# A relative-position bias table in SBUF: loaded at another place in GpSimd's queue, straight into its own buffer

## The chip, the core and the metric

The kernel runs on one core of one Trainium2 chip. The time is device microseconds (us) of one execution of the whole program; a measurement gives the median of several runs. The engines are TensorE (PE; its weight loads are PEld), VectorE (DVE), ScalarE (ACT), GpSimd (POOL) and SyncE (SP), each with its own instruction stream, tied together by semaphores. DMAs are issued by SP (queue q1 in the profile) and by GpSimd (queue q0), and both are carried by the same 16 DMA engines of the core.

## What is computed

One decoder block on x of 256 tokens x 1024: a normalised input is projected by `w_in`, two token mixers run in parallel on the projections, and their outputs are gated, merged and projected again. The change touches the bias of the second mixer:

```
dist_own = qpos[:, None] - (own_start + offs)[None, :]
s_own = einsum('bhcd,bhkd->bhck', qc, k_own) + bias_hb[:, t5_bucket(dist_own)][None]
s_own = where(dist_own >= 0, s_own, NEG_INF)
```

The bias of head h for query i and key j depends on i - j alone. So a row of 384 values for each head (`bias_rows` in DRAM, with -1e30 where i < j) holds all of it, and partition p of the table is that row from element p on: 256 ascending values, which have to be read from the last to the first to be in the order of the keys.

The first mixer (gated DeltaNet, 8 heads) needs, for every head and each of two chunks of 128 tokens, the inverse of a unit lower-triangular matrix; its blocks of 32 x 32 are solved by a substitution on DVE, over all heads at once.

## The kernel before

**Tiles.** All weights go through four slots (`raw`, `w_hi`, `w_lo`, each 128 x 1024). A tile is 512 KB. SP loads it into `raw` (L387), ACT rounds it to `w_hi` (L636), DVE makes the remainder `w_lo` (L865), and PE multiplies in three thirds: high by high, high weight by low input, low weight by high input (L1274 for most tiles, L1292 for the value tiles), some 0.96 us a third. One counter S numbers the thirds of the whole program, tile n having S = 3n, 3n+1, 3n+2; every engine's program is unrolled along S by hand, so each engine works strictly in the order that its own code has.

**Loads.** Tiles are loaded in pairs: SP waits for `s_lo` before an even tile n, that is until `w_lo` of tile n-3 is made, and then issues n and n+1. ACT casts tile n+2 during part 1 of tile n (`split_hi`), DVE makes its `w_lo` in part 2 (`split_lo`). Tiles 0 to 15 are key (K) and value (V) tiles; a K tile is fetched in rows of 512 B.

**Around the change.** For each key tile, ACT copies the product (L687), DVE adds three taps (L938), ACT takes the tanh (L690), DVE finishes `kT_all` (L951); then `key_tokens(j)` lets PE transpose it (L1340) and ACT square and copy it (L699, L701). `key_tokens(j)` on PE waits until ACT has copied that of j-1 (`s_k0`). At S = 26 to 33 ACT runs `decay`, 16 exponentials over `th_E` (L678); at S = 28 to 39 `similarity` on PE (L1351) and DVE (L964) writes `la_all`, which is the memory of `xin`.

**GpSimd.** It stores the bias rows (L539) and the decay rows (L541) to DRAM, loads the bias table into `xin` under the name `climbing` (L544, 1 MB), loads the decay rows broadcast to all partitions into `th_E` in two halves (L548, 512 KB each), computes the norms of the first keys, masks the first half of `th_E` (L495), copies `climbing` with reversed columns into `bias` (L555), and masks the second half. DVE waits for that copy (`s_bias`) before its first write of `la_all`. Later GpSimd stores and loads the blocks of the substitution (L504, L513), computes the value norms (L488), and waits for the substitution's end (L569). The table is first read by DVE at L1043 and L1045 in `stage_a` of head 0, at S = 99.

Of the kernel before, what the change touches and what calls it, by code (L numbers as in the profile page):

```python
# [31 lines left out]
P = 128  # L32
HALF = P // 2
D = 1024
SEQ = 256
NC = SEQ // P
KT = D // P
HEADS = 8
# [3 lines left out]
SCALE = float(P) ** -0.5  # L42
# [45 lines left out]
BIAS_W = 384  # L88
# [20 lines left out]
def build(nc, x, norm_pre_w, w_in, b_gate, conv_w, dn_a_log, dn_dt_bias, dn_onorm_w, rel_bias, w_branch, w_out,  # L109
          norm_post_w, consts, onehot, out):  # L110
    with ExitStack() as ctx:
        def sb(name, shape, dt=F32):
            return ctx.enter_context(nc.sbuf_tensor(name, shape, dt))

        def sem(name):
            return ctx.enter_context(nc.semaphore(name))
# [3 lines left out]
        bA, bB, bC, bD, bE, bF = bank[2:]  # L120
# [4 lines left out]
        xin = sb("xin", [P, NC, D])  # L125
# [13 lines left out]
        bias = sb("bias", [P, HEADS, SEQ])  # L139
# [33 lines left out]
        sc = sb("sc", [P, BIAS_W])  # L173
# [19 lines left out]
        E_all = th_E[:, late:late + HEADS, :].rearrange("p h (c n) -> p h c n", c=NC)  # L193
        E_flat = th_E[:, late:late + HEADS, :].rearrange("p h n -> p (h n)")
        la_all = xin[:].rearrange("p c n -> p (c n)").rearrange("p (h c n) -> p h c n", h=HEADS, c=NC)
        climbing = xin[:].rearrange("p c n -> p (c n)").rearrange("p (h n) -> p h n", h=HEADS)
        m2, m32 = acc, tacc[:, 0, :]
        squares = T_all[:].rearrange("p h c n -> p (h c n)")[:, 0:512]
        post = vtok_all[:, 0, :]
# [5 lines left out]
        bias_rows = nc.dram_tensor("bias_rows", [HEADS, BIAS_W], F32, kind="Internal").ap()  # L205
# [31 lines left out]
        s_M_in2 = sem("s_M_in2")  # L237
        s_M_out2 = sem("s_M_out2")
        s_G_p = sem("s_G_p")
        s_M_in = sem("s_M_in")  # L240
# [15 lines left out]
        s_bias = sem("s_bias")  # L256
        s_bias_p = sem("s_bias_p")
        s_brow = sem("s_brow")
        s_climb = sem("s_climb")
        s_cst = sem("s_cst")  # L260
        s_d_p = sem("s_d_p")
        s_f = sem("s_f")
# [10 lines left out]
        s_hT = sem("s_hT")  # L273
# [63 lines left out]
        s_stored = sem("s_stored")  # L337
# [99 lines left out]
        def _(pool):  # L437
# [47 lines left out]
            def value_norms(q):  # L485

                heads = slice(2 * q, 2 * q + 2)
                pool.tensor_tensor(tab[:, 2:4, heads], tk[:, 0, :, heads], power[:, 0], ALU.pow).then_inc(s_vn, 1)  # L488
                pool.wait_ge(s_vn, q + 1)

            def mask_decay(half):

                pool.wait_ge((s_E_in, s_E_in2)[half], 16)
                part = E_all[:, 4 * half:4 * half + 4].rearrange("p h c n -> p (h c) n")
                pool.affine_select(part, part, [[0, 4 * NC], [1, P]], ALU.is_ge, NEG_INF, base=0,  # L495
                                   channel_multiplier=-1).then_inc(s_Em, 1)
                pool.wait_ge(s_Em, half + 1)
# [41 lines left out]
            pool.dma_start(bias_rows, brow).then_inc(s_stored, 16)  # L539
            pool.wait_ge(s_grow, 1)  # L540
            pool.dma_start(g_rows, grow[:]).then_inc(s_g_out, 16)  # L541
            pool.wait_ge(s_stored, 16)
            pool.wait_ge(s_hT, KT)
            pool.dma_start(climbing, bass.AP(bias_rows.tensor, 0, [[1, P], [BIAS_W, HEADS], [1, SEQ]])).then_inc(s_climb, 16)  # L544
            pool.wait_ge(s_g_out, 16)
            for half in range(2):
                size = HEADS * SEQ // 2
# [3 lines left out]
            pool.wait_ge(s_tab, 2)  # L551
            norms(0)
            mask_decay(0)
            pool.wait_ge(s_climb, 16)
            pool.tensor_copy(bias[:], climbing[:, :, SEQ - 1::-1]).then_inc(s_bias, 1)  # L555
            pool.wait_ge(s_bias, 1)
            mask_decay(1)
            norms(1)
            norms(2)
# [4 lines left out]
            load_blocks(1)  # L564
            for q in range(HEADS // 2):
                value_norms(q)
            pool.wait_ge(s_sub, 2 * STEPS)
            for a in range(2):
                pool.dma_start(bass.AP(t_blocks.tensor, BLK * a, [[BLK * BLK, HALF], [2 * BLK, BLK // 2], [1, BLK]]),  # L569
# [286 lines left out]
        def _(ve):  # L856
            v = nc.vector
# [30 lines left out]
            for k in range(KT):  # L888
                ve.wait_ge(s_h_hi, k + 1)
                v.scalar_tensor_tensor(out=h_lo[:, k, :], in0=bank[k][:, 0:SEQ], scalar=vec[:, R_PRE + k:R_PRE + k + 1],  # L890
                                       in1=h_hi[:, k, :].bitcast(F32), op0=ALU.mult, op1=ALU.subtract).then_inc(s_h_lo, 1)
# [61 lines left out]

            def similarity(j):

                if j == 0:
                    ve.wait_ge(s_bias, 1)
                if j % 2 == 0:
                    ve.wait_ge(s_sig, j + 1)
                ve.wait_ge(s_E, 2 * j + 2)  # L960
                ve.wait_ge(s_G_p, j + 1)
                for c in range(NC):
                    ps = (bA, bC)[j % 2][:, P * c:P * c + P]
                    v.scalar_tensor_tensor(out=la_all[:, j, c, :], in0=ps, scalar=tab[:, c, j:j + 1],  # L964
                                           in1=E_all[:, j, c, :], op0=ALU.mult, op1=ALU.mult).then_inc(s_la, 1)
# [64 lines left out]
            def stage_a(g, s):  # L1030
                at = at2[:, g % 2]
                if s == 14:
                    ve.wait_ge(s_A_p, g + 1)
                    if g >= 2:
                        ve.wait_ge(s_o1_p, g - 1)
                    v.tensor_tensor(at, chunks(bA[:, 0:256]), E_all[:, g], ALU.mult).then_inc(s_A, 1)
                elif s == 15:
                    ve.wait_ge(s_sc_p, g + 1)
                    if g == 0:
                        ve.wait_ge(s_bias, 1)  # L1040
                    if g:
                        ve.wait_ge(s_pt_p, g)
                    v.scalar_tensor_tensor(out=sc[:, 0:256], in0=bC[:, 0:256], scalar=SCALE, in1=bias[:, g, :],  # L1043
                                           op0=ALU.mult, op1=ALU.add).then_inc(s_sc, 1)
                    v.scalar_tensor_tensor(out=sc[:, 256:384], in0=bC[:, 256:384], scalar=SCALE, in1=bias[:, g, P:2 * P],  # L1045
                                           op0=ALU.mult, op1=ALU.add).then_inc(s_sc, 1)
                    ve.wait_ge(s_sc, 2 * g + 1)
                    v.tensor_reduce(mx[:, 0:1], sc[:, 0:256], AX_X, ALU.max).then_inc(s_mx, 1)
                    ve.wait_ge(s_sc, 2 * g + 2)
                    v.tensor_reduce(mx[:, 1:2], sc[:, 256:384], AX_X, ALU.max).then_inc(s_mx, 1)  # L1050
                    ve.wait_ge(s_mx, 2 * g + 2)
                    v.tensor_scalar(mx[:, 2:4], mx[:, 0:2], -1.0, None, ALU.mult).then_inc(s_nmx, 1)
                elif s == 18:
                    ve.wait_ge(s_pexp, 2 * g + 2)
                    v.reciprocal(mx[:, 6:8], mx[:, 4:6]).then_inc(s_rsum, 1)
                elif s == 25:
                    ve.wait_ge(s_pv_p, g + 1)
                    ve.wait_ge(s_gz, 2 * g + 2)
                    if g:
                        ve.wait_ge(s_ylo_b, g)  # L1060
                    v.scalar_tensor_tensor(out=y32[:, 1, :], in0=bA[:, 0:SEQ], scalar=0.5, in1=gzb[:],
                                           op0=ALU.mult, op1=ALU.mult).then_inc(s_yb32, 1)
                elif s == 27:
                    ve.wait_ge(s_yhi_b, g + 1)
                    v.tensor_tensor(y_lo[:, 1, g:g + 1, :], one(y32[:, 1, :]),
                                    y_hi[:, 1, g:g + 1, :].bitcast(F32), ALU.subtract).then_inc(s_ylo_b, 1)
# [66 lines left out]
            for S in range(3 * BRANCH0):  # L1133
                n, part = S // 3, S % 3
# [19 lines left out]
            with ve.Fori(0, KT // 2) as i:  # L1154
                for t in range(4):
# [4 lines left out]
                    if t % 2 == 0:  # L1160
                        ve.wait_ge(s_m_hi, d + 1)
                    v.scalar_tensor_tensor(out=one(m2[:, t % 2, :]), in0=(th_a if t % 2 else th_b)[:, bass.ds(d, 1), :],
                                           scalar=1.0, in1=one(bank[t % 2][:, 0:SEQ]), op0=ALU.add,
# [11 lines left out]
            for c in range(NC):  # L1175
# [7 lines left out]
                for e in range(2):  # L1183
                    cols = slice(512 * e, 512 * e + 512)
                    v.scalar_tensor_tensor(out=res[:, c, cols], in0=res[:, c, cols], scalar=tiny[:, 30 + c:31 + c],
                                           in1=raw[:, c, cols], op0=ALU.mult, op1=ALU.add).then_inc(s_o_f, 1)
# [350 lines left out]
```

## Time and profile before

| | us |
|---|---|
| median of 3 runs (375.31 to 375.71) | 375.61 |
| the profiled execution, its own time | 374.69 |
| its span in the trace | 372.9 |
| busy: PE / PEld | 359.8 / 344.8 |
| busy: DVE / ACT / POOL | 268.9 / 219.2 / 62.4 |
| granted TensorE clock, mean | 0.994 |

The trace counts from its first record; 1.8 us of the execution's own time lie outside the span. A line such as L636 is line 636 of the kernel. Busy time of an engine is that of its instructions, without the issuing of DMAs on SP. The granted clock is given in parts of 2.4 GHz: 1.00 is 2.4 GHz, 0.50 is 1.2 GHz.

### The profile page before, as it was taken

The numbers are of one execution on the slowest core, as the hardware profiler recorded it, in microseconds if no ns is written. First come the engines' busy times: TensorE is split into PE (matmuls) and PEld (weight loads), VectorE is DVE, ScalarE is ACT, GpSimd is POOL, SyncE is SP. The second block draws the span as 40 slices with busy tenths as digits, with TensorE's granted clock in tenths as the row PEclk, the third lists the DMA queues.
The fourth block names the chain that finished last, engine by engine and source line by source line (L and its number), as shares of the span: only waits on it lengthen the run. The fifth ranks groups of instructions, "written<-read, shape, count | busy, mean of one in ns | idle before, by whom it ended". The sixth has DMA issues, their size and how long they took to land.

```text
span 372.9 us, 7655 instructions
## 1 busy us (share of the span) xinstructions
PE 359.8 (96%) x2755; PEld 344.8 (92%) x2755; DVE 268.9 (72%) x558; ACT 219.2 (59%) x500; POOL 62.4 (17%) x121
## 2 busy tenths in 40 slices
PE   8999599999999999999999999999999999999993
PEld 6788597799999999999999999999999999999882
DVE  2966595479966887878878878688786557667644
ACT  5783696444556566767666586666676643534531
POOL 3544415550033000202020201001020100000000
PEclk9999899999999999999999999999999999999999
DMA  8849645976787654484447544466446565765533
GB/s 259 219 129 284 200 146 147 239 199 152 190 228 186 173 150 114 124 212 120 114 119 193 143 112 115 122 179 153 112 117 182 155 183 156 212 208 199 224 116 113
DMA packets 99343, 62.45 MB, mean 167 GB/s; under 512 B 3652, under 2 KB 94190, under 8 KB 99310
## 3 DMA queue, kind: packets, MB, share of 16 engines
q1 hardware_dynamic: 98014, 58.59, 56.9%
q0 software_dynamic: 1296, 3.43, 3.2%
q8 instruction: 20, 0.33, 0.4%
q14 instruction: 13, 0.11, 0.1%
HBM read 60.41 MB, written 1.59 MB: 166 GB/s over the span
## 4 chain that ended last, share of the span: by engine, by line
PE 88%; DMA 4%; ACT 4%; DVE 2%; issue 1%; POOL 1%; DVEq 0%; POOLq 0%; ACTq 0%
PE banks L1274 63%; PE banks L1491 6%; PE banks L1292 4%; DMA raw<-in_w_in_dram 3%; ACT th_E L678 1%; PE banks L1374 1%; PE banks L1259 1%; PE banks L1381 1%; PE banks L1392 1%; DMA xin<-in_x_dram 1%; PE banks L1430 1%; PE banks L1219 1%; ACT junk L699 1%; PE banks L1433 1%; PE banks L1437 0%
## 5 line engine op out<-in xcount | busy, mean ns | idle before, releaser
L865 DVE TENSOR_TENSOR w_lo<-raw,w_hi 128x1024 fp32r<-128x1024 f32 x102 | 124.5, 1223 | 37.6 <-ACT w_hi L636 37.4
L636 ACT CAST w_hi<-raw 128x1024 fp32r<-128x1024 f32 x103 | 106.6, 1045 | 13.2 <-DMA raw<-in_w_in_dram 7.8
L1274 PE MATMUL banks<-h_lo,w_hi 128*128 128x256 f32 x568 | 83.1, 289 | 0.0
L1274 PE MATMUL banks<-h_hi,w_lo 128*128 128x256 f32 x568 | 82.8, 289 | 0.0
L1274 PE MATMUL banks<-h_hi,w_hi 128*128 128x256 f32 x568 | 82.1, 287 | 0.3 <-PE banks L1292 0.3
L1274 PEld LDWEIGHTS banks<-h_hi,w_hi 128*128 128x128 f32 x568 | 72.7, 191 | 1.4 <-issue 1.4
L1274 PEld LDWEIGHTS banks<-h_lo,w_hi 128*128 128x128 f32 x568 | 73.5, 193 | 0.0
L1274 PEld LDWEIGHTS banks<-h_hi,w_lo 128*128 128x128 f32 x568 | 73.3, 192 | 0.0
L938 DVE SCALAR_TENSOR_TENSOR acc<-banks,vec,acc 128x255 f32<-128x255 f32 (+2 forms) x72 | 34.5, 479 | 6.0 <-ACT acc L734 3.3
L586 POOL TENSOR_TENSOR so<-so,rnq 128x2 f32<-128x2 f32 x8 | 3.8, 471 | 148.8 <-ACT junk L801 148.8
L845 ACT CAST h_hi<-tacc 128x256 f32 x8 | 3.2, 406 | 28.4 <-DVE tacc L1167 28.4
L742 ACT ACTIVATE tz<-banks 128x256 f32<-128x256 f32 x16 | 6.1, 384 | 22.7 <-PE banks L1274 22.7
L1274 PE MATMUL banks<-y_hi,w_hi 128*128 128x256 f32 x128 | 18.0, 283 | 0.0
L1274 PE MATMUL banks<-y_lo,w_hi 128*128 128x256 f32 x128 | 18.0, 283 | 0.0
L1274 PE MATMUL banks<-y_hi,w_lo 128*128 128x256 f32 x128 | 18.0, 283 | 0.0
L1274 PEld LDWEIGHTS banks<-y_hi,w_hi 128*128 128x128 f32 x128 | 16.5, 192 | 0.0
L1274 PEld LDWEIGHTS banks<-y_hi,w_lo 128*128 128x128 f32 x128 | 16.5, 192 | 0.0
L1274 PEld LDWEIGHTS banks<-y_lo,w_hi 128*128 128x128 f32 x128 | 16.5, 192 | 0.0
L734 ACT ACTIVATE acc<-banks,vec 128x256 f32<-128x256 f32 x16 | 7.6, 473 | 15.0 <-PE banks L1274 14.9
L1491 PE MATMUL banks<-w_hi,h_hi 128*128 128x512 f32 x32 | 12.5, 389 | 0.0
L1491 PE MATMUL banks<-w_lo,h_hi 128*128 128x512 f32 x32 | 12.5, 389 | 0.0
L1491 PE MATMUL banks<-w_hi,h_lo 128*128 128x512 f32 x32 | 12.4, 389 | 0.0
(243 smaller groups left out, 546.6 us busy)
## 6 DMA issues: line engine op xcount, KB each, us to landing
raw<-in_w_in_dram SPq DMA_DIRECT2D x80, 512.0 KB, 5.2
raw<-in_w_branch_dram SPq DMA_DIRECT2D x16, 512.0 KB, 4.8
raw<-in_w_out_dram SPq DMA_DIRECT2D x8, 512.0 KB, 4.1
xin<-in_x_dram SPq DMA_DIRECT2D x2, 512.0 KB, 3.7
xin<-bias_rows POOLq DMA_DIRECT2D x1, 1024.0 KB, 7.3
th_E<-g_rows POOLq DMA_DIRECT2D x2, 512.0 KB, 8.2
raw<-in_x_dram SPq DMA_DIRECT2D x2, 512.0 KB, 4.1
out_dram<-xin SPq DMA_DIRECT2D x4, 256.0 KB, 2.0
```

Of the source, the lines that this page charges most:

```text
L586: pool.tensor_tensor(so[:, 2:4], so[:, 0:2], rnq[:, g % 2, :], ALU.add).then_inc(s_f, 1)
L636: nc.scalar.copy(w_hi[:, t % SLOTS, :], raw[:, t % SLOTS, :]).then_inc(s_hi, 1)
L678: ac(E_all[:, h, c, :], E_all[:, h, c, :], ACT.Exp, bias=ng[:, c, h:h + 1]).then_inc(s_E, 1)
L699: ac(junk[:, 0:P], ps[:, P * c:P * c + P], ACT.Square, accum_out=ssqk[:, c, j:j + 1]).then_inc(s_ksq, 1)
L734: ac(acc[:, t, :], ps, ACT.Copy, scale=tap(CONV - 1, 2 * t, h)).then_inc(s_tap0, 1)
L742: ac(tz[:, t - 4, :], ps, ACT.Tanh, scale=0.5).then_inc(s_tz, 1)
L865: v.tensor_tensor(w_lo[:, t % SLOTS, cols], raw[:, t % SLOTS, cols], w_hi[:, t % SLOTS, cols].bitcast(F32), ALU.subtract).then_inc(s_lo, 1)
L938: v.scalar_tensor_tensor(out=acc[:, a, i:], in0=ps[:, 0:SEQ - i], scalar=tap(CONV - 1 - i, w, h), in1=acc[:, a, i:], op0=ALU.mult, op1=ALU ...
L1219: last = mm(bA[0:4 * HEADS, 0:SEQ], wbd2[:, k, :], h_part[:, k, :], start=k == 0 and h_part is h_hi, stop=k == KT - 1 and h_part is h_lo)
L1274: last = mm(ps, w, r, start=part == 0 and k == 0, stop=part == 2 and k == KT - 1)
L1292: last = mm(((bE, bF), (bB, bE))[group][c], left, right, start=q == 0 and kk == 0 and part == 0, stop=q == 3 and kk == 1 and part == 2)
L1491: last = mm(bank[2 + 2 * c + e], m[:, k, P * c:P * c + P], w[:, (OUT0 + k) % SLOTS, 512 * e:512 * e + 512], start=k == 0 and m is m_hi and ...
```

## The change

GpSimd no longer issues the load of the bias table between the store of the decay rows and their load; the wait for `s_hT` goes with it. The reversing copy on GpSimd between the two masks is gone, and so is DVE's wait for it before `la_all` is written. Instead GpSimd issues one load of the same bytes, in the same pattern, into `bias` itself. It stands behind the value norms, behind waits for the rows' store and for the landing of the substitution's blocks (`s_M_in`, `s_M_in2`), and ahead of the wait for the substitution's end. DVE's 16 reads of the table (two for each of 8 heads) now run with reversed columns, and `s_bias` counts to 16.

```
-            pool.wait_ge(s_stored, 16)
-            pool.wait_ge(s_hT, KT)
-            pool.dma_start(climbing, bass.AP(bias_rows.tensor, 0, [[1, P], [BIAS_W, HEADS], [1, SEQ]])).then_inc(s_climb, 16)
             pool.wait_ge(s_g_out, 16)
...
             mask_decay(0)
-            pool.wait_ge(s_climb, 16)
-            pool.tensor_copy(bias[:], climbing[:, :, SEQ - 1::-1]).then_inc(s_bias, 1)
-            pool.wait_ge(s_bias, 1)
             mask_decay(1)
...
             for q in range(HEADS // 2):
                 value_norms(q)
+            pool.wait_ge(s_stored, 16)
+            pool.wait_ge(s_M_in, 32)
+            pool.wait_ge(s_M_in2, 32)
+            pool.dma_start(bias[:], bass.AP(bias_rows.tensor, 0, [[1, P], [BIAS_W, HEADS], [1, SEQ]])).then_inc(s_bias, 16)
             pool.wait_ge(s_sub, 2 * STEPS)
...
-                if j == 0:
-                    ve.wait_ge(s_bias, 1)
                 if j % 2 == 0:
                     ve.wait_ge(s_sig, j + 1)
...
                     if g == 0:
-                        ve.wait_ge(s_bias, 1)
+                        ve.wait_ge(s_bias, 16)
...
-                    v.scalar_tensor_tensor(out=sc[:, 0:256], in0=bC[:, 0:256], scalar=SCALE, in1=bias[:, g, :],
+                    v.scalar_tensor_tensor(out=sc[:, 0:256], in0=bC[:, 0:256], scalar=SCALE, in1=bias[:, g, SEQ - 1::-1],
...
-                    v.scalar_tensor_tensor(out=sc[:, 256:384], in0=bC[:, 256:384], scalar=SCALE, in1=bias[:, g, P:2 * P],
+                    v.scalar_tensor_tensor(out=sc[:, 256:384], in0=bC[:, 256:384], scalar=SCALE, in1=bias[:, g, P - 1::-1],
```

GpSimd's instructions from the store of the bias rows to the second mask, before. `xin` in the third row is `climbing`, `tk` and `tab` are the norms of the first keys.

```order
L539 DMA bias_rows<-pt 8x384 [waits s_brow,s_gs]
L541 DMA g_rows<-grow 8x256 [waits s_grow]
L544 DMA xin<-bias_rows 128x8x256 [waits s_hT,s_stored]
L548 DMA th_E<-g_rows 128x1024 [waits s_g_out]
L548 DMA th_E<-g_rows 128x1024
L476 TENSOR_SCALAR tk<-ssqk 128x2x2 [waits s_ksq,s_tab]
L478 TENSOR_TENSOR tk<-tk,power 128x2x2 [waits s_nk]
L480 TENSOR_TENSOR tab<-tk,gt 128x2x2 [waits s_nk]
L482 TENSOR_TENSOR tab<-tab 128x2 [waits s_sig]
L495 AFFINE_SELECT th_E<-th_E 128x1024 [waits s_E_in,s_sig]
L555 COPY bias<-xin 128x2048 [waits s_climb,s_Em]
L495 AFFINE_SELECT th_E<-th_E 128x1024 [waits s_E_in2,s_bias]
```

The same stretch now (line numbers of the changed kernel):

```order
L537 DMA bias_rows<-pt 8x384 [waits s_brow,s_gs]
L539 DMA g_rows<-grow 8x256 [waits s_grow]
L543 DMA th_E<-g_rows 128x1024 [waits s_g_out]
L543 DMA th_E<-g_rows 128x1024
L474 TENSOR_SCALAR tk<-ssqk 128x2x2 [waits s_ksq,s_tab]
L476 TENSOR_TENSOR tk<-tk,power 128x2x2 [waits s_nk]
L478 TENSOR_TENSOR tab<-tk,gt 128x2x2 [waits s_nk]
L480 TENSOR_TENSOR tab<-tab 128x2 [waits s_sig]
L493 AFFINE_SELECT th_E<-th_E 128x1024 [waits s_E_in,s_sig]
L493 AFFINE_SELECT th_E<-th_E 128x1024 [waits s_E_in2,s_Em]
```

One DMA of 1 MB and one copy have left this stretch. The DMA stands further down on the same engine, between the value norms (`tab<-tk,power`) and the stores that follow the substitution:

```order
L486 TENSOR_TENSOR tab<-tk,power 128x2x2
L486 TENSOR_TENSOR tab<-tk,power 128x2x2 [waits s_vn] x3
L562 DMA bias<-bias_rows 128x8x256 [waits s_M_in,s_M_in2,s_stored,s_vn]
L565 DMA t_blocks<-sub 1024x1x32 [waits s_sub]
L565 DMA t_blocks<-sub 1024x1x32
```

Before, the two stores (L569) stood directly behind the value norms (L488). No other engine's instructions have moved.

## Rows read from the trace of the kernel before

**Rows 1.** The page: span, busy time, and where the last chain ran.
```profile
span 372.9 us, 7655 instructions
...
PE 359.8 (96%) x2755; PEld 344.8 (92%) x2755; DVE 268.9 (72%) x558; ACT 219.2 (59%) x500; POOL 62.4 (17%) x121
```

**Rows 2.** Windows: busy us of each engine (instructions), granted clock, DMA share, GB/s.
```profile
38.00:40.00 2.00, 0.00 (x0) 0.00 (x0) 0.00 (x0) 0.95 (x2) 1.85 (x2) 1.00 1.13 328
42.00:44.00 2.00, 2.00 (x11) 2.00 (x11) 1.96 (x3) 1.20 (x7) 0.00 (x0) 0.50 0.09 25
50.00:55.00 5.00, 4.99 (x36) 4.42 (x35) 4.50 (x13) 4.94 (x20) 1.05 (x2) 1.00 0.23 48
85.00:90.00 5.00, 5.00 (x44) 5.00 (x43) 4.79 (x10) 2.63 (x4) 0.00 (x0) 1.00 0.83 210
```

**Rows 3.** Timeline of PE: start, us, what, [idle before and its releaser].
```profile
41.06 0.66 PE L1340 MATMUL banks<-cst,kT_all 128*128 128x128 f32 x2 [3.91 <-ACT k_all L701]
...
43.22 1.60 PE L1274 MATMUL banks<-h_hi,w_lo 128*128 128x256 f32 x8
44.65 1.11 PE L1274 MATMUL banks<-h_hi,w_hi 128*128 128x256 f32 x8
...
57.24 0.41 PE L1340 MATMUL banks<-cst,kT_all 128*128 128x128 f32 x2 [0.37 <-ACT k_all L701]
...
90.37 1.12 PE L1274 MATMUL banks<-h_hi,w_hi 128*128 128x256 f32 x8
```

**Rows 4.** Timeline of ACT.
```profile
39.05 1.04 ACT L636 CAST w_hi<-raw 128x1024 fp32r<-128x1024 f32 x1 [5.32 <-DMA raw<-in_w_in_dram]
...
43.96 0.26 ACT L701 COPY k_all<-banks 128x128 f32<-128x128 f32 x1
44.86 0.47 ACT L687 ACTIVATE acc<-banks,vec 128x256 f32<-128x256 f32 x1 [0.64 <-PE banks L1274]
...
46.91 0.42 ACT L690 ACTIVATE tacc<-acc 128x256 f32<-128x256 f32 x1 [0.65 <-DVE acc L938]
```

**Rows 5.** SP's loads issued at 27.8 and 28.2, and their landing.
```profile
L387 SPq DMA_DIRECT2D raw<-in_w_in_dram x2: 368/495/622, 27.8 to 28.2; - x2
...
DMA to landing us min/median/max: 11.2/11.9/12.6
```

**Rows 6.** DMA queues from 31 to 32 and from 34 to 35: packets, MB, share.
```profile
q0 software_dynamic: 54, 0.22, 80.5%
q1 hardware_dynamic: 54, 0.03, 17.4%
...
q0 software_dynamic: 99, 0.36, 87.1%
q1 hardware_dynamic: 99, 0.05, 16.7%
```

**Rows 7.** Timeline of GpSimd.
```profile
27.16 0.95 POOL L544 DMA_DIRECT2D xin<-bias_rows  x1
28.55 1.08 POOL L548 DMA_DIRECT2D th_E<-g_rows  x2 [0.43 <-DMA g_rows<-grow]
74.11 5.59 POOL L488 TENSOR_TENSOR tab<-tk,power 128x4 f32<-128x4 f32 x4
```

**Rows 8.** SP's loads issued at 78.9 and 79.3, and ACT's cast of the first.
```profile
L387 SPq DMA_DIRECT2D raw<-in_w_in_dram x2: 368/866/1365, 78.9 to 79.3; - x2
...
DMA to landing us min/median/max: 4.0/4.9/5.8
...
85.18 1.04 ACT L636 CAST w_hi<-raw 128x1024 fp32r<-128x1024 f32 x1
```

**Rows 9.** The inverse's last loads, its first use on DVE, and the table's reads.
```profile
109.99 2.60 POOL L574 DMA_DIRECT2D T_all<-t_blocks  x4 [3.46 <-DMA t_blocks<-sub]
...
L1043 DVE SCALAR_TENSOR_TENSOR sc<-banks,bias x8: 391/418/425, 123.0 to 281.6; 128x256 f32<-128x256 f32 x8
...
122.68 0.44 DVE L1076 STREAM_TRANSPOSE sub<-T_all 128x256 f32<-128x256 f32 x1
```

More of the change, by code:

```diff
@@ L195, in build @@
         la_all = xin[:].rearrange("p c n -> p (c n)").rearrange("p (h c n) -> p h c n", h=HEADS, c=NC)
-        climbing = xin[:].rearrange("p c n -> p (c n)").rearrange("p (h n) -> p h n", h=HEADS)
         m2, m32 = acc, tacc[:, 0, :]
@@ L258, in build @@
         s_brow = sem("s_brow")
-        s_climb = sem("s_climb")
         s_cst = sem("s_cst")
```

## The prediction, made before the changed kernel ran

> **What bounds the kernel now.** I read the page first. PE is busy for 96% of the span [rows 1], so a change can win only where PE stands still or runs slowly, and lose only where it makes PE wait. The windows then show one such place in the whole first third: from 38 to 40 PE does nothing at all while the DMA engines are full, and from 42 to 44 it works at a granted clock of 0.50, its lower level of 1.2 GHz, after this standstill [rows 2]. The timeline of PE gives the sizes: an idle time of 3.91 us, ended by an ACT copy of key tokens (L701), and then 2.16 us (41.06 to 43.22) for two transposes and a third and 1.43 us (43.22 to 44.65) for the next third [rows 3]. At full clock these would take some 0.3 + 0.96 + 0.96 = 2.2 us instead of 3.59 (a third is 0.96 us; see the description of the kernel), so the slow clock costs 1.4 us. The hole is worth 3.9 + 1.4 = 5.3 us in all.
>
> The timeline of ACT says who is behind it. ACT itself sat for 5.32 us, until 39.05, for a weight tile to land; ACT works in order, so the copy that PE wants stands behind this cast [rows 4]. The tile was issued at 27.8 and took 11.2 us to land, its pair 12.6 us [rows 5]; the same kind of pair at 78.9 takes 4.0 and 5.8 us [rows 8]. The DMA queues tell why. From 31 to 32 GpSimd's queue q0 moved 54 packets and 0.22 MB, SP's q1 54 packets and 0.03 MB; from 34 to 35 it was 99 packets and 0.36 MB against 99 packets and 0.05 MB [rows 6]. The queues take turns packet by packet, and a packet of q0 is 4 KB (0.22 MB over 54) where one of the key tile is 512 B. So as long as q0 has work, the weight tile hardly moves. What q0 had is 2 MB: the bias table, issued at 27.16, and the decay rows, issued from 28.55 [rows 7]. The change takes the first of these two away from here.
>
> **What the load's removal gives.** The table is 1 MB or 256 packets of 4 KB, and goes first. At 54 packets per us it holds the queue for 256 / 54 = 4.7 us. Without it the decay rows can't start at once: they wait for their own store and are issued 28.55 - 27.16 = 1.4 us later than the table was [rows 7]. So q0 is empty 4.7 - 1.4 = 3.3 us sooner. In that time the tile would have moved a little even so (0.03 MB per us [rows 6]), and needs the time for it afterwards: 3.3 us x 0.03 = 0.1 MB, at the 328 GB/s that the engines reach behind q0 [rows 2] 0.3 us. That leaves 3.0; I take **2.9 us**, since 54 packets per us is the rate in the middle of the load and its end may be faster. The lower bound: if the slow rate of 54 belongs to whatever comes first and not to the table's pattern, the decay rows take 256 / 54 = 4.7 us instead of 256 / 99 = 2.6, and 2.1 of the 3.3 us are lost: 1.2 us. The upper bound is the standstill itself: 3.9 us.
>
> The Trainium skill, "DMA: Bandwidth & Descriptors", section "Anatomy of one DMA — SWDGE (gpsimd) path", gives such a DMA about 2.0 us fixed and bytes / 436e3 us more. By that page the removed transfer holds the engines for an estimated 2.4 us, and the sum below would be about 3.0 us instead of 3.5. The trace differs, 0.22 MB in a us for the table's packets [rows 6], and I go by it.
>
> So the tile lands near 36.1 instead of 39.0, and PE, which is there at 41.06 - 3.91 = 37.15 [rows 3], still stands for 3.9 - 2.9 = 1.0 us. The clock was full until the end of the long standstill and full through all short ones, so I expect it to stay at 1.00 after this one.
>
> **Who is next.** That frees 2.9 + 1.4 = 4.3 us for PE, but PE isn't alone. From 46.91 ACT has no gap: tanh, 16 decays, casts and token copies; it is busy for 4.94 of the 5 us from 50 to 55 [rows 2], and at 57.24 PE waits for it again, 0.37 us [rows 3]. What counts after that is how much earlier ACT gets to its tanh at 46.91. It is carried forward by the tile's 2.9 us. It also had two waits on the way: 0.64 us for PE's slow thirds before the copy at 44.86, and 0.65 us for DVE's taps, which hang on that copy [rows 4]. The first goes, since with a full clock the product is finished before ACT has ended its token copy at 43.96 + 0.26; the second stays, since the taps follow the copy at the same distance. So ACT is 2.9 + 0.6 = **3.5 us** early, PE's surplus of 0.8 us becomes a longer wait near 57 - 3.5, and from there everything is 3.5 us early.
>
> **The other parts.** The reversing copy on GpSimd (1.9 us by its place between the masks) is off every path: the masks are done before 41, and the first decay is at 47, behind ACT's own queue [rows 4]. The wait of DVE at its first write of `la_all`, near 49.7, was long over; it goes at no gain. The waits for `s_stored` and `s_M_in` at the new place are satisfied: GpSimd is in its value norms from 74.11 for 5.59 us [rows 7], and what is queued behind the new DMA waits for the substitution anyway (the inverse's loads come at 109.99 [rows 9]). The issue itself, 0.95 us at L544 [rows 7], falls in that idle time.
>
> DVE's reads with reversed columns: the trace has no such read on DVE. Below, no change of 0.418 us each [rows 9]; above, twice that, 0.4 us for each of 16 reads. GpSimd's own reversed copy ran at about the speed of its plain fills, so I take no change; and 0.4 us twice in a head's 17 us of PE work doesn't reach PE, since DVE is idle a quarter of the time. Zero, with 0.3 us in the range.
>
> **The load at its new place.** It is issued at 74.11 + 5.59 - 3.5 = 76.2. SP's pair of 78.9 is then issued at 75.4 and meets it. That pair lands 4.0 and 5.8 us after its issue when alone [rows 8]; held up by 256 packets at 99 to 54 per us, 2.6 to 4.7 us, it lands after 6.6 to 8.7 and 8.4 to 10.5 us. ACT casts the first tile 85.18 - 78.9 = 6.3 us after issue [rows 8], so ACT and DVE may wait up to 2.4 us. PE wants it at 90.37 [rows 3]: less 1.05 for the cast and 0.5 for ACT's gate tanh in between, landing may take 9.9 us, and 2.9 us more for the second. 1.2 us are left, so I cost this at nothing; without that cover it costs what lands beyond 9.9. The lost turns are regained slowly, since the engines are 83% busy there [rows 2], but a pair is issued only when slots are free, so the delay doesn't add up. DVE, 4.79 of 5 us busy [rows 2], may end the substitution 2.4 us later; the inverse's loads at 109.99 + 2.60 land some 4 us later, near 116.5, and are wanted at 122.68 [rows 9]. That covers it too.
>
> The rule of the Trainium skill that speaks against the change is in the same page, "Issuing engines are not separate DMA queues": DMAs of all issuing engines run on the same 16 DMA engines and interleave. By it the moved megabyte is only paid elsewhere; that is the third rival, and the packets of [rows 6] agree that it interleaves.
>
> **Sum.** Profiled execution 374.69 - 3.5 = 371.2; the median of the runs stands 0.92 above that execution, 375.61 - 3.5 = **372.1 us**.
>
> **Rivals.** *The whole hole closes* (18%). The tile lands before 35, or ACT's row of work isn't as tight as it looks: 375.61 - 5.3 = 370.3. For it: a tile lands in 4 us when alone. Against it: the decay rows still hold q0, and ACT's 4.94 of 5 us.
>
> *The decay rows alone hold the tile nearly as long* (15%). At 54 packets per us the gain is 1.2 + 0.6 = 1.8: 373.8. If the queue is slower still, or PE's clock falls all the same after 2 to 3 us of standstill (1.4 us minus), it ends at 374.9 or above, within 0.2% of before; I give this last part 6 of the 15.
>
> *The load starves the weights at its new place* (5%). If the pair of 78.9 lands as late as that of 27.8 did, 12.6 us [rows 5], it is 12.6 - 9.9 = 2.7 us too late for PE: 375.61 - 3.5 + 2.7 = 374.8. It decides against the change once `w_lo`, and with it SP's next pair, is late too: twice 2.7 is 5.4, more than 3.5, and gives 377.5. Against it: only half of q0's bytes are there.
>
> *The table comes too late for DVE at 123* is out: issued at 76.2, it would have to take over 40 us.
>
> **How the numbers follow.** Forecast 62%, the rivals 18, 15 and 5. A difference below 0.2%, 0.75 us, is about what a measurement can't tell from none. Faster: 62 + 18 + 9 = 89%; same 6%; slower 5%. The range goes from 369.9, the whole hole with half a us beyond it, to 374.3, the second rival's 373.8 with 0.5 for the reads and the new place; it leaves out the same and slower cases and a little at the fast end.
>
> **What will show it.** Right: the pair of 27.8 lands in 8 to 9 us; ACT waits about 2.4 us for it instead of 5.3; PE's standstill at 37 is about 1 us and no window near 42 shows a clock under 1; PE waits over 1 us near 54; DVE's reads stay at 0.42 us; ACT waits for `raw` once or twice from 80 to 86, and PE doesn't. Wrong: a pair that still takes 10 us or more at 27.8, a clock of 0.5 anywhere, or PE idle between 78 and 95.

## The result, and the profile after

| | before | after |
|---|---|---|
| median, us (lowest to highest) | 375.46 (374.52 to 375.71) | 369.72 (369.47 to 369.83) |
| the profiled execution, us | 374.69 | 369.6 |
| its span, us | 372.9 | 367.8 |
| mean granted clock | 0.994 | 0.996 |

The ratio is 0.985, 95% interval 0.983 to 0.987: the changed kernel is 5.7 us faster. (One execution of 1240.42 us, disturbed, is left out of its median.) A second measurement gave 369.54 (369.37 to 369.68) against 375.14 (374.41 to 376.07), ratio 0.985 [0.983, 0.987]. The forecast was 372.1, in a range from 369.9 to 374.3: the sign and the place are right, and the gain is 5.7 us where 3.5 were predicted. The time lies just below the range, next to the 370.3 of the rival that the whole hole closes.

The page shows a span 5.1 us shorter, of which 1.8 us are busy time that PE no longer has ([rows 1]; it was not doing more work before, but the same work at half clock):

```profile
span 367.8 us, 7652 instructions
...
PE 358.0 (97%) x2755; PEld 343.1 (93%) x2755; DVE 269.2 (73%) x558; ACT 219.3 (60%) x500; POOL 60.6 (16%) x120
```

SP's pair that is issued at 28.0 (27.8 in [rows 5]); the last line is the time from issue to landing:

```profile
L385 SPq DMA_DIRECT2D raw<-in_w_in_dram x2: 367/475/583, 28.0 to 28.4; - x2
...
DMA to landing us min/median/max: 4.3/6.1/8.0
```

4.3 us instead of 11.2: the tile is there at 32.3, 6.7 us earlier, not 2.9. The DMA queues from 30 to 31, 31 to 32, 32 to 33 and 33 to 34 (packets, MB, share of the engines) show what changed:

```profile
q1 hardware_dynamic: 628, 0.32, 109.3%
...
q1 hardware_dynamic: 660, 0.33, 113.9%
...
q1 hardware_dynamic: 305, 0.16, 60.3%
q0 software_dynamic: 44, 0.18, 54.7%
...
q0 software_dynamic: 85, 0.33, 91.1%
q1 hardware_dynamic: 84, 0.04, 14.6%
```

From 29 until 32 SP's queue has the engines alone, with 0.32 and 0.33 MB in its last two us against 0.03 before [rows 6]. The decay rows were issued at 28.68 on GpSimd's queue q0, and no packet of theirs comes before 32.1. Once both queues move, they take turns here too (85 packets against 84 from 33 to 34). This is the timeline of GpSimd (start, us, what, [idle before and its releaser]):

```profile
28.68 1.12 POOL L543 DMA_DIRECT2D th_E<-g_rows  x2 [1.37 <-DMA g_rows<-grow]
...
69.28 5.30 POOL L486 TENSOR_TENSOR tab<-tk,power 128x4 f32<-128x4 f32 x4
...
74.88 0.96 POOL L562 DMA_DIRECT2D bias<-bias_rows  x1 [0.30 <-POOL tab L486]
...
105.48 2.61 POOL L570 DMA_DIRECT2D T_all<-t_blocks  x4 [3.98 <-DMA t_blocks<-sub]
```

ACT's cast of that tile, which waited 5.32 us before [rows 4], waits for nothing. It starts 5.31 us earlier, so 1.4 of the tile's 6.7 us are not used; the tanh of 46.91 comes 5.14 us earlier. ACT's timeline:

```profile
33.74 1.06 ACT L632 CAST w_hi<-raw 128x1024 fp32r<-128x1024 f32 x1
...
41.77 0.42 ACT L686 ACTIVATE tacc<-acc 128x256 f32<-128x256 f32 x1 [0.81 <-DVE acc L934]
```

PE's timeline, where the hole was [rows 3]:

```profile
37.12 0.38 PE L1334 MATMUL banks<-cst,kT_all 128*128 128x128 f32 x2
...
39.25 1.12 PE L1268 MATMUL banks<-h_hi,w_hi 128*128 128x256 f32 x8
...
46.52 0.41 PE L1334 MATMUL banks<-cst,kT_all 128*128 128x128 f32 x2 [0.25 <-ACT k_all L697]
...
52.10 0.41 PE L1334 MATMUL banks<-cst,kT_all 128*128 128x128 f32 x2 [0.36 <-ACT k_all L697]
```

The transposes that stood 3.91 us until 41.06 run at 37.12 without a wait. The high by high third of 44.65 is at 39.25, 5.40 us earlier: the standstill and the 1.4 to 1.5 us of the slow clock. Then 0.25 us go back into a new wait at 46.52, and from the transposes of 57.24, now 52.10, on PE is 5.1 us early, to the end of the span. The windows from 38 to 40 and 42 to 44 (busy us of PE, PEld, DVE, ACT, POOL; granted clock, DMA share, GB/s) answer [rows 2]:

```profile
38.00:40.00 2.00, 2.00 (x19) 2.00 (x19) 2.00 (x3) 1.55 (x8) 1.25 (x2) 1.00 0.31 117
42.00:44.00 2.00, 2.00 (x20) 2.00 (x19) 1.97 (x4) 2.00 (x8) 0.00 (x0) 1.00 0.97 341
```

At the new place the table is issued at 74.88, behind SP's pair of 73.7 and 74.2, which is the pair of 78.9 of the kernel before. Its first tile lands after 4.5 us and its second after 9.4, at 83.6; the next pair, of 79.6, lands after 5.8 and 6.9 us. ACT waits for one of the four, the second tile of the pair of 73.7, for 0.53 us, and PE doesn't wait. DVE's reads with reversed columns take 0.416 us, where the plain ones took 0.418 [rows 9]:

```profile
L385 SPq DMA_DIRECT2D raw<-in_w_in_dram x2: 368/1154/1940, 73.7 to 74.2; - x2
...
DMA to landing us min/median/max: 4.5/6.9/9.4
...
83.58 1.05 ACT L632 CAST w_hi<-raw 128x1024 fp32r<-128x1024 f32 x1 [0.53 <-DMA raw<-in_w_in_dram]
...
L1037 DVE SCALAR_TENSOR_TENSOR sc<-banks,bias x8: 386/416/426, 117.9 to 276.5; 128x256 f32<-128x256 f32 x8
```

### The profile page after: what moved, and what is told of

Same layout as the page of the kernel before. It is cut to its first block, busy times and chain, and to the rows that moved or that the text cites. A ratio compares the mean times of both kernels' runs of the same rounds, so it can differ in the third digit from the quotient of the medians.

```text
span 367.8 us, 7652 instructions
## 1 busy us (share of the span) xinstructions
PE 358.0 (97%) x2755; PEld 343.1 (93%) x2755; DVE 269.2 (73%) x558; ACT 219.3 (60%) x500; POOL 60.6 (16%) x120
## 4 chain that ended last, share of the span: by engine, by line
PE 84%; DVE 6%; ACT 5%; issue 2%; DMA 1%; POOL 1%; DVEq 0%; POOLq 0%; ACTq 0%
PE banks L1268 63%; PE banks L1485 6%; PE banks L1286 4%; DVE acc L934 2%; DVE w_lo L861 2%; ACT th_E L674 1%; PE banks L1368 1%; PE banks L1375 1%; PE banks L1386 1%; DMA xin<-in_x_dram 1%; ACT h_hi L646 1%; ACT w_hi L632 1%; PE banks L1424 1%; ACT junk L695 1%; PE banks L1427 1%
## 5 line engine op out<-in xcount | busy, mean ns | idle before, releaser
L861 DVE TENSOR_TENSOR w_lo<-raw,w_hi 128x1024 fp32r<-128x1024 f32 x102 | 124.7, 1225 | 32.5 <-ACT w_hi L632 32.2
L1268 PE MATMUL banks<-h_lo,w_hi 128*128 128x256 f32 x568 | 82.2, 287 | 0.0
L1268 PEld LDWEIGHTS banks<-h_lo,w_hi 128*128 128x128 f32 x568 | 72.7, 191 | 0.0
L1485 PE MATMUL banks<-w_hi,h_hi 128*128 128x512 f32 x32 | 12.5, 389 | 0.0
L1485 PE MATMUL banks<-w_lo,h_hi 128*128 128x512 f32 x32 | 12.5, 389 | 0.0
```

The source lines that it names most:

```text
L861: v.tensor_tensor(w_lo[:, t % SLOTS, cols], raw[:, t % SLOTS, cols], w_hi[:, t % SLOTS, cols].bitcast(F32), ALU.subtract).then_inc(s_lo, 1)
L1268: last = mm(ps, w, r, start=part == 0 and k == 0, stop=part == 2 and k == KT - 1)
L1485: last = mm(bank[2 + 2 * c + e], m[:, k, P * c:P * c + P], w[:, (OUT0 + k) % SLOTS, 512 * e:512 * e + 512], start=k == 0 and m is m_hi and ...
```

## The experiments

Two theories of the larger gain were open. *Order*: the pair of 28.0 goes fast because it finds the engines free, and whoever is on them first keeps the other away. *Bytes*: the pair goes fast because q0 has 1 MB less. A third was that the new wait-free path (copy and DVE's wait dropped) has a part in it. The first four runs were made on one chip beside 19 runs of before, median 374.94.

**The same bytes, the other order.** The kernel before, with the table's load behind the two loads of decay rows:

```
-            pool.wait_ge(s_stored, 16)
-            pool.wait_ge(s_hT, KT)
-            pool.dma_start(climbing, ...).then_inc(s_climb, 16)
             pool.wait_ge(s_g_out, 16)
             for half in range(2):
...
+            pool.wait_ge(s_stored, 16)
+            pool.wait_ge(s_hT, KT)
+            pool.dma_start(climbing, ...).then_inc(s_climb, 16)
             pool.wait_ge(s_tab, 2)
```

> The kernel before with one change: the table's load is issued behind the two decay-row loads instead of ahead of them; the copy on GpSimd and all bytes stay. Theory 'who arrives first': the weight pair issued at 28 gets to the engines before any packet of the decay rows (in the changed kernel q1 moved 0.93 MB from 29 to 33 and q0's first packets came at 32.1), so only a transfer that is already there can hold it up. Then the pair lands in 4 to 8.5 us, PE has no standstill at 37 and the time is 369.7 to 370.5, though q0 carries 2 MB as before. Theory 'bytes' (the prediction's): q0's megabytes decide; with all 2 MB still there the pair lands in about 11 us and the time is 375 to 376.

Measured: 372.33 (371.07 to 373.17), ratio 0.991 [0.988, 0.995]. The pair of 28.0 lands after 4.0 and 8.4 us and PE doesn't stand at 37: with all 2 MB still in q0, the first hole is gone. So it is the order that opens or closes the hole, and not the bytes. But the time is 1.8 us above the range that this theory expected. The next pair, issued at 33.8 and 34.2 into the full q0, lands after 8.4 and 9.3 us. ACT, PE, and the window from 50 to 51:

```profile
42.18 1.05 ACT L636 CAST w_hi<-raw 128x1024 fp32r<-128x1024 f32 x1 [2.10 <-DMA raw<-in_w_in_dram]
...
48.86 0.41 PE L1340 MATMUL banks<-cst,kT_all 128*128 128x128 f32 x2 [2.53 <-ACT k_all L701]
...
50.00:51.00 1.00, 1.00 (x4) 0.81 (x4) 0.96 (x3) 0.97 (x7) 0.00 (x0) 0.50 0.32 39
```

The wait of 2.53 us at PE (0.25 in the changed kernel) has two sources. In the changed kernel ACT waits 0.81 us for DVE before the tanh of 41.77, so only 1.3 of the 2.10 us make it late. The rest comes over DVE: the table lands late, GpSimd's copy and second mask move to 41.82 and 43.86, and DVE's `w_lo` and `kT_all`, which now run beside them, take 1.53 and 1.30 us where they take 1.22 and 0.42 alone. ACT's next tanh waits for that:

```profile
47.48 0.42 ACT L690 ACTIVATE tacc<-acc 128x256 f32<-128x256 f32 x1 [0.88 <-DVE acc L938]
```

A slow clock follows. The expectation had priced one pair only, and nothing of the copy.

**The changed kernel with the load at its old place**, directly into `bias`; no copy, no wait of DVE, reversed reads.

```
             pool.dma_start(g_rows, grow[:]).then_inc(s_g_out, 16)
+            pool.wait_ge(s_stored, 16)
+            pool.wait_ge(s_hT, KT)
+            pool.dma_start(bias[:], ...).then_inc(s_bias, 16)
```

(the same load, with its waits, goes from the place behind the value norms.)

> The changed kernel with its table load back at the old place, ahead of the decay rows, still straight into its own buffer and read with reversed columns, without the copy on GpSimd. Both theories: the move alone does it, so 375.2 to 375.8 and the pair of 27.8 lands in 11 to 12.6 us. A rival, that the dropped copy and the dropped wait bring part of the gain, expects 372 to 374.

Measured: 374.71 (374.33 to 375.52), ratio 0.9987 [0.9976, 0.9999]. The pair lands after 11.2 and 12.5 us, and PE stands as before:

```profile
41.18 0.41 PE L1333 MATMUL banks<-cst,kT_all 128*128 128x128 f32 x2 [3.92 <-ACT k_all L696]
```

So the gain is the load's move. Dropping the copy and the wait is worth 0.2 us by the medians and at most 0.9 by the interval, as long as the hole is there. What keeping the copy would cost once the hole is closed is not shown by it.

**The changed kernel without any load of the table.** It leaves the load and its wait out, so the bias that is added is whatever the memory holds.

```
-            pool.dma_start(bias[:], ...).then_inc(s_bias, 16)
...
-                    if g == 0:
-                        ve.wait_ge(s_bias, 16)
```

> The changed kernel without the table's load at all (the bias that is added is then what the buffer holds; left out is the bias). It prices the load at its new place. The prediction's costing, nothing: within 0.3 us of the changed kernel, 369.4 to 370.0. Rival 'collision', the load costs PE something near 80: 0.8 us or more faster than the changed kernel.

Measured: 369.62 (369.43 to 369.72), ratio 0.985 [0.983, 0.987], within 0.1 us of the 369.72 and 369.54 of the changed kernel. No cost of the moved megabyte at its new place shows.

**The changed kernel with the pair held until both halves of `th_E` have landed.** This leaves the decay rows alone on the engines.

```
                     sp.wait_ge(s_lo, n)
+                    if isinstance(n, int) and n == 8:
+                        sp.wait_ge(s_E_in2, 16)
```

> The changed kernel, but SP issues the pair of tiles 8 and 9 only when the decay rows have landed. The decay rows then run on engines that carry nothing else. Theory 'the pair's stream held q0 back': their first packets come 1.6 us after issue, as the table's did in the kernel before, they land by 34, the pair by 38.5, ACT waits 4 to 5 us, time about 373.5. Theory 'this form of load starts late whatever else runs': first packets 3.4 us after issue again, landing near 35.5, the pair near 40, PE stands for 4 to 5 us and its clock falls to 0.5: 375.5 to 377.

Measured: 374.62 (372.82 to 375.09), ratio 0.997 [0.996, 0.999]. The decay rows were issued at 28.84. q0 has no packet from 29 to 30, and this from 30 to 31:

```profile
q0 software_dynamic: 65, 0.27, 70.0%
```

With free engines its first packets come 1.3 us after the issue, and the table's came after 1.6 before (27.16 to some 28.8). In the changed kernel the same load needed 3.4 us. DVE and ACT do the same work in both runs from 28 to 33, so the pair of SP is all that differs: it is no latency of this kind of load, it is the running pair that holds q0 back. The pair of 34.2 then came too late for ACT (5.44 us), and PE stood for 4.03 us.

**The pair one tile later.** With 30.8 as its issue, it meets decay rows that are already under way, which is the order that the prediction had assumed for 27.8.

```
-                    sp.wait_ge(s_lo, n)
+                    sp.wait_ge(s_lo, 9 if isinstance(n, int) and n == 8 else n)
```

> The changed kernel, but SP issues the pair of tiles 8 and 9 one tile later (behind the remainder of tile 6, near 30.9 instead of 28.0). So the decay rows are on the engines first (from 30.2 when nothing else runs) and the table isn't there: just the state that the prediction assumed for the changed kernel. Theory 'who arrives first': the pair is held up like in the prediction's sum, it lands near 36.3, PE stands about 1 us at 37, no clock falls, and the time is 2 to 2.5 us above the changed kernel, 371.5 to 372.3. Theory 'the prediction's sum itself was wrong even with the decay rows ahead': the pair lands in 4 to 5.5 us, before 36, and the time stays within 0.4 of the changed kernel.

This run and the next three were made beside 19 runs of before, median 374.77. Measured: 371.75 (371.73 to 371.79), ratio 0.992 [0.990, 0.994]. The pair lands after 5.5 and 7.1 us, at 36.3, where the prediction had put the tile at 36.1. ACT and PE:

```profile
36.35 1.05 ACT L632 CAST w_hi<-raw 128x1024 fp32r<-128x1024 f32 x1 [2.53 <-DMA raw<-in_w_in_dram]
...
38.37 0.41 PE L1334 MATMUL banks<-cst,kT_all 128*128 128x128 f32 x2 [1.12 <-ACT k_all L697]
...
54.31 0.41 PE L1334 MATMUL banks<-cst,kT_all 128*128 128x128 f32 x2 [0.38 <-ACT k_all L697]
```

Predicted were 2.4 and 1.0 us, and a clock that stays at 1.00, which it does. The transposes of 57.24 come 2.93 us earlier, 3.5 were summed. Given its order, the sum is good to 0.6 us. The DMA queues from 31 to 32, 32 to 33 and 33 to 34:

```profile
q0 software_dynamic: 44, 0.18, 97.5%
...
q0 software_dynamic: 104, 0.36, 95.3%
...
q0 software_dynamic: 75, 0.25, 61.4%
q1 hardware_dynamic: 223, 0.11, 37.6%
```

The pair of 30.8 has no packet before 33. Here it is SP's queue that gets nothing until q0 is nearly done. So the order is the assumed one and the sharing isn't: the sum had both queues take turns, and gave the tile 0.03 MB a us in them. That the tile lands within 0.2 us of the predicted 36.1, from an issue 3 us later, is in this part luck.

**The pair two tiles later**, issued at 33.7: the same line with 10 in place of 9.

> The changed kernel, but SP issues the pair of tiles 8 and 9 two tiles later (behind the remainder of tile 7, near 33.8), when the decay rows, alone on the engines, are done. It lands near 37.8 and PE stands 2.5 to 3 us at 37. It asks what a standstill of that length does to the clock: if the clock needs about 3.7 us of standstill to fall, as in the kernel before (37.15 to 40.9), it stays at 1.00 and the time is 371.9 to 372.6; if it falls, 373.3 or more.

Measured: 373.41 (372.42 to 375.85), ratio 0.996 [0.994, 0.997]. It landed after 5.8 us, later than reckoned, and three loads were issued from 33.7 to 34.8; ACT waited 5.73 and PE 4.32 us. The time goes with the mean granted clock of the run, from 372.42 to 372.49 us at 0.998 to 375.85 at 0.986. In the profiled one, the slowest, PE resumes at 41.57, and the windows from 40 to 46 are:

```profile
40.00:42.00 2.00, 0.43 (x3) 0.46 (x3) 1.36 (x2) 1.97 (x8) 0.00 (x0) 0.50 0.74 273
42.00:44.00 2.00, 2.00 (x12) 2.00 (x11) 1.93 (x4) 1.35 (x4) 0.00 (x0) 0.50 0.04 16
44.00:46.00 2.00, 2.00 (x11) 2.00 (x11) 0.82 (x2) 0.90 (x5) 1.28 (x2) 0.50 0.21 17
```

Here the clock fell earlier in the standstill than in the kernel before, where the expectation had taken 3.7 us as what it needs: it was 0.76 in the us from 39 and 0.50 in the next, against 1.00 and 0.94 before.

**Twice and three times the load at the new place.** Further copies of the same 1 MB, directly behind the table's, into a buffer that is free by then. This measures how far the cover reaches.

```
             pool.dma_start(bias[:], ...).then_inc(s_bias, 16)
+            pool.dma_start(y_lo[:, 0].bitcast(F32), ...).then_inc(s_extra0, 16)
+            pool.dma_start(y_lo[:, 1].bitcast(F32), ...).then_inc(s_extra1, 16)
```

(the last line only in the second of them; DVE waits for the extra loads where it waits for `s_bias`.)

> The changed kernel with a second load of the same 1 MB behind the table's at the new place (into memory that is written much later). It tests the margin there. The prediction's sum: one load uses up to 2.4 us of ACT's lead and leaves PE 1.2 us, so a second one, 3 to 4.7 us more, makes the pair issued near 80 land after 11 to 13 us and costs PE 0.5 to 3 us: 370.2 to 372.7. Theory 'who arrives first': the pair issued near 74 is ahead of both loads, the pair near 80 meets their end only, and the cost is at most 1 us: 369.5 to 370.6.

> The same with two loads behind the table's, 3 MB in all. Both theories: the pair issued near 80 now stands behind 6 us and more of GpSimd's packets and lands after 12 us or more, ACT waits over 4 us, PE stands still near 88 to 91 and the time is 372 to 377; if PE doesn't stand even here, the new place was never a risk.

Measured: 370.12 (369.67 to 370.40) with 2 MB, ratio 0.988 [0.986, 0.990], and 373.29 (370.94 to 375.55) with 3 MB, ratio 0.996 [0.993, 0.999]. Against the two medians of the changed kernel that is some 0.5 and 3.7 us. With 2 MB, as in the changed kernel, it is the second tile of the pair ahead of the loads (73.5 and 73.9) that is hit first: it lands after 12.7 us, at 86.6; the next pair, of 79.3, lands after 9.1 and 10.1. ACT waits 3.85 us for the tile of 73.9 and 0.38 for that of 79.3, yet PE is busy for 2.93 of the 3 us from 88 to 91. In the profiled execution with 3 MB the value norms took longer and the loads were issued at 75.80, 1.2 us later than with 2 MB. The pair of 73.6 lands untouched after 4.1 and 5.8 us, and all of the weight falls on the pair of 79.4: it lands after 12.0 and 13.3 us, and PE waits. The first line is with 2 MB, the others with 3:

```profile
86.60 1.05 ACT L635 CAST w_hi<-raw 128x1024 fp32r<-128x1024 f32 x1 [3.85 <-DMA raw<-in_w_in_dram]
...
91.39 1.04 ACT L636 CAST w_hi<-raw 128x1024 fp32r<-128x1024 f32 x1 [5.63 <-DMA raw<-in_w_in_dram]
...
92.86 0.38 PE L1274 MATMUL banks<-h_hi,w_hi 128*128 128x256 f32 x1 [1.86 <-ACT th_a L716]
```

The prediction's limits were 9.9 us for the first tile of a pair and 9.9 + 2.9 = 12.8 for the second, and both hold. With 2 MB the second tile lands 86.6 - 73.5 = 13.1 us after its pair's issue, 0.3 too late by the sum; PE's third is 0.23 late. With 3 MB the first lands 12.0 - 9.9 = 2.1 too late by the sum, and PE waits 1.86. The slow clock behind that wait costs another 1.6 us (three thirds take 4.47 us instead of 2.88).

**The kernel before, with the table's load issued 1.4 us later.** Only one wait of GpSimd is moved ahead of it; order, bytes and place in the queue stay; the decay rows behind it are issued 0.9 us later (29.45).

```
             pool.dma_start(g_rows, grow[:]).then_inc(s_g_out, 16)
+            pool.wait_ge(s_g_out, 16)
             pool.wait_ge(s_stored, 16)
             pool.wait_ge(s_hT, KT)
             pool.dma_start(climbing, ...).then_inc(s_climb, 16)
-            pool.wait_ge(s_g_out, 16)
```

> The kernel before with one wait moved: GpSimd waits for the decay rows' store before it issues the table's load, not after. Order and bytes of its queue stay (table, then decay rows); the table is only issued some 1.4 us later, at 28.6 instead of 27.2, and so just behind SP's pair of 28.0. Theory 'who arrives first': this 1.4 us alone lets the pair go ahead: the first tile lands in 4 to 5 us and PE has no standstill at 37; what is lost is lost later, at the next pair, as with the load behind the decay rows: 370.5 to 373. Theory 'bytes': as before, 374.5 to 375.8, and the tile lands in 11 us. On what is open, the late start of q0's packets behind a running pair: if it is a property of the decay rows' form, the table's first packets come near 30.2; if the running pair holds any load back, near 32.

Measured: 370.84 (370.71 to 371.34) against 375.14, ratio 0.989 [0.987, 0.991]. The table's issue, SP's pair, and the DMA queues from 32 to 33 and 33 to 34:

```profile
28.51 0.96 POOL L545 DMA_DIRECT2D xin<-bias_rows  x1 [1.38 <-DMA g_rows<-grow]
...
L387 SPq DMA_DIRECT2D raw<-in_w_in_dram x2: 367/475/583, 27.8 to 28.2; - x2
...
DMA to landing us min/median/max: 4.0/4.9/5.8
...
q1 hardware_dynamic: 412, 0.20, 84.6%
q0 software_dynamic: 29, 0.12, 39.1%
...
q0 software_dynamic: 81, 0.33, 99.3%
q1 hardware_dynamic: 3, 0.00, 0.5%
```

The first packets of q0 come at 32.5, 4.0 us after the issue, and the pair has landed by 34.0. So the form of the load doesn't matter either: both loads of GpSimd that were issued behind the running pair waited for it, and the table issued 1.4 us earlier took most of the engines for itself. What is left to the changed kernel is the second pair. Issued at 33.6, behind the running q0, it has no packet from 34 to 37 and lands after 8.4 us; ACT waits 2.13 us for it, and PE 1.52:

```profile
47.82 0.41 PE L1340 MATMUL banks<-cst,kT_all 128*128 128x128 f32 x2 [1.52 <-ACT k_all L701]
```

4.3 of the 5.6 us that the changed kernel gains on this chip come with one moved wait and no byte less.

## Why the prediction was wrong, point by point

**What bounds the kernel** was right: the hole at 37 to 45, with the weight tile behind ACT and ACT behind PE. It is what closed, and the rest of the span is unchanged but for its start.

**"What the load's removal gives" is the step that failed.** It says that the decay rows, "issued from 28.55", take over q0 where the table was, so that q0 is merely empty 3.3 us sooner, and gives the term 2.9 us. That assumes that the decay rows are on the engines ahead of the pair as the table had been. But the pair is issued at 28.0, before them; only the table, at 27.16, was ahead of it. I read the two rows of issue, 27.16 and 28.55 [rows 7], and the row of SP, 27.8 [rows 5], and didn't put them in one order. In place of 2.9 the tile's landing moved by 6.7 us, from 39.0 to 32.3, of which ACT's cast used 5.31. The run with the pair one tile later restores the assumed order, and there the term is 2.70 (cast 39.05 to 36.35) and the median 371.75, near the forecast of 372.1. The condition of the lower bound is half met there: without a table before them the decay rows move 57 and 44 packets in the us from 30 and 31, and 104 only then.

The term for PE's slow thirds was small as well: 0.6 us of ACT's waiting, of 1.4. Even with the upper bound of 3.9 us for the tile the sum would have been 4.5. Without the standstill PE has its third of 44.65 5.40 us early and ACT its tanh 5.14, so nearly all of the slow clock's 1.4 us went with it.

The prediction's premise that the queues take turns packet by packet was read from a stretch in which q0 had come first [rows 6]. The Trainium skill has the same rule ("DMA: Bandwidth & Descriptors", section "Queues, rings and completion order": each DMA engine goes round between the queues that have work, a packet at a time). The trace agrees with it in [rows 6], 54 packets against 54, and in the changed kernel from 33 to 34, 85 against 84. It doesn't account for the 3.4 us from 28.68, in which the decay rows have been issued and move nothing; whether their packets were already at the engines then, no row shows.

**"Who is next"** was right in kind and cautious in size. ACT's row of work is nearly tight: of the 2.13 us by which a tile was late for ACT with the table 1.4 us later, 1.27 came out at PE (1.52 against 0.25), and 0.81 went into a wait for DVE that ACT had anyway. PE does wait for ACT afterwards, but 0.25 us new and 0.36 as before, not over 1 us: ACT moved by 5.14, near to what PE could use.

**The execution against the median.** The forecast took the median 0.92 us above the profiled execution. That distance belonged to the hole. Among the 47 runs of before that the experiments brought, the 20 with a mean clock of 0.986 or 0.987 took 375.1 to 376.1 us, and those with 0.990 or more 374.3 to 375.2: by that, the stretch at half clock is not equally long in each. Without the standstill it is gone (369.6 and 369.72). So 0.8 of the 2.4 us between forecast and result lie here, and 1.6 in the profiled execution itself (371.2 against 369.6).

**The parts costed at nothing** held. Copy and wait: at most 0.9 us, 0.2 by the medians. Reversed reads: 0.416 against 0.418 us. The new place: 0.1 us or less, ACT waits once, PE never. The pair of 78.9, now of 73.7, was expected to land after 6.6 to 8.7 and 8.4 to 10.5 us and took 4.5 and 9.4. The limits of 9.9 and 12.8 us were confirmed by 3 and 2 MB. The table took longer than a price on paper, though: the Trainium skill, "DMA: Bandwidth & Descriptors", section "Anatomy of one DMA — SWDGE (gpsimd) path", gives 2.0 us and bytes / 436e3, an estimated 4.4 us for 1 MB; here it landed after 7.3 us, beside SP's loads. It had 40 us.

**Two sums are off**, and neither moves the forecast. With the 2.4 us that the prediction takes from the Trainium skill in place of its 4.7, its own steps give 2.4 - 1.4 = 1.0 us for the queue and, with the 0.6 of ACT, an estimated 1.5 in all; the 3.0 leaves out the 1.4. And half a us beyond the whole hole is 370.3 - 0.5 = 369.8, not 369.9; the 369.72 lies beyond either.

**The rivals.** That the whole hole closes (18%) is what happened, by its first condition, "the tile lands before 35" (32.3); what had spoken for it, that a tile lands in 4 us when alone, was the case, and against it I had held the decay rows, which weren't there yet. The decay rows alone hold the tile: no, unless the pair is made to come behind them. The load starves the weights: only with three times its bytes does PE wait for over 1 us.

**Its signs.** Right: reads at 0.42, one wait of ACT in 80 to 86, no wait of PE from 78 to 95, no window near 42 with a clock under 1. Wrong: landing in 8 to 9 us (4.3), ACT's 2.4 us (0), PE's 1 us at 37 (0), over 1 us near 54 (0.36). The first of these would have told the failed step by itself.

No run was faster than the changed kernel by more than its own two medians differ (369.72 and 369.54).

## What to carry to other kernels

Before you count the bytes that two queues share, put the issues of both in one order: which transfer is on the engines first decided more here (a 1.4 us later issue of the same bytes was worth 4.3 us) than how much there was. Price the next pair of loads too, not only the one that you free, and count its lateness at the next engine in full, less the waits that the engine in between has anyway. Look also at what the other engines then do side by side: GpSimd's copy and mask were free in the standstill, and beside DVE's work they held ACT up by 0.9 us in the swapped order. And take a median from one profiled execution with care where the time differs with the length of a slow-clock stretch that the change removes.

## What the runs showed of the hardware

**Who comes first keeps the engines for a while.** First packets of q0 came 1.3 to 1.6 us after the issue on free engines (the table before; the decay rows with the pair held), and 3.4 and 4.0 us behind a running pair of SP. In the other direction, a pair issued at 30.8 behind a running q0 had no packet until 33, and in the last experiment SP's queue moved 3 packets in the us from 33 and none from 34 to 37, with a pair issued at 33.6. Yet at the new place q0's first packets came 1.8 us after the issue, with SP's pair of 73.7 still under way (10 packets from 76 to 77, 53 in the next us beside 31 of SP's), and in the kernel before both alternate. What tells these cases apart is open: that it is how much of SP's pair is already queued at the issue would be an argument, and no run tested it.

**The clock and the length of a standstill.** After waits of PE of 1.12 and 1.52 us the granted clock stayed at 1.00. After 1.86 us (3 MB) and 2.53 us (the swapped order) it was at 1.00 when PE resumed and fell to 0.50 within the next 2 us. With 3 MB, PE resumes at 92.86, and the windows are:

```profile
92.00:93.00 1.00, 0.14 (x1) 0.14 (x2) 0.53 (x1) 0.81 (x2) 0.00 (x0) 1.00 1.20 290
93.00:94.00 1.00, 1.00 (x8) 1.00 (x9) 0.97 (x3) 0.81 (x1) 0.00 (x0) 0.81 1.20 290
94.00:95.00 1.00, 1.00 (x7) 1.00 (x7) 0.90 (x4) 0.61 (x2) 0.00 (x0) 0.50 1.17 281
```

After 3.91 us (before) and 4.32 (the pair two tiles later) it was at 0.50 already when PE resumed; after 3.92 us (the load at its old place) it was at 1.00 in the us from 40, PE resumed at 41.18, and the next two us had 0.85 and 0.50; after 4.03 us (the pair held) it was 1.00 in the us of the resumption and 0.62 in the next. So a standstill half as long as the one that I had found cost clock too, once it came, and the same length didn't always give the same clock. The prediction had allowed for that in a part of one rival, and no more.

**DVE beside GpSimd.** In the swapped order DVE's `w_lo` (128 x 1024) and `kT_all` (128 x 256) took 1.53 and 1.30 us where GpSimd's copy and mask ran, against 1.22 and 0.42 elsewhere, and GpSimd's mask 1.89 us against 1.09. In the changed kernel the `w_lo` of 38.30, beside the masks, took 1.68.
